# Second block's mixers: the recurrence between the projections, norm statistics per tile, norm weights in the columns, the FFN result per bank

## The reference

```
for layer in 0, 1:
    sh1, sc1, g1, sh2, sc2, g2 = split(silu(c) @ ada_w + ada_b)
    u = x * (1 + sc1) + sh1
    c_b, c_c, c_h, q, k, v, g, g_low = split(u @ w_in)        # 512 x3, 256 x2, 512 x2, 16
    y_conv = c_b * causal_conv3(c_c * c_h)
    gk = max(log_sigmoid(g_low @ gk_w2 + gk_b) / 16, -1);  b = cumsum(gk) in chunks of 64
    o  = (q e^b)(k e^-b)^T v, causal in the chunk, + (q e^b) state of the chunks before
    y_gla = rms(o) * gla_norm_w * silu(g)
    x = layernorm(alpha * x + (1 + g1) * [y_conv, y_gla] @ w_out) * ln1_g + ln1_b
    u = x * (1 + sc2) + sh2
    ff = dense SwiGLU, 2816 wide (layer 0)  or  8 experts of 2816, top 2 (layer 1)
    x = layernorm(alpha * x + (1 + g2) * ff) * ln2_g + ln2_b
```

## Time and profile before

| | us |
|---|---|
| median of 3 runs (lowest, highest) | 2401.27 (2396.63, 2406.88) |
| profiled execution, its own time | 2399.09 |
| its span | 2397.3 |
| layer 0's mixer, first transposes to first FFN matmul | 909.8 to 1094.5 |
| layer 0's FFN and norm, to the next transposes | 1094.5 to 1348.6 |
| layer 1's mixer, to the router | 1348.6 to 1536.0 |
| layer 1's experts, to the end | 1536.0 to 2397.3 |

### The profile page before, as it was taken

One profiled execution on the slowest core, in us unless ns is written; L12 is line 12 of the kernel. 1 busy time (PEld: TensorE's weight loads), 2 busy tenths in 40 slices (PEclk: granted clock), 3 DMA queues, 4 the chain that ended last, 5 costly groups with the idle time before them and its releaser, 6 DMA issues.

```text
span 2397.3 us, 68445 instructions
## 1 busy us (share of the span) xinstructions
PE 2180.4 (91%) x31915; PEld 1793.0 (75%) x31915; DVE 694.5 (29%) x1496; ACT 141.8 (6%) x270; POOL 160.6 (7%) x196
## 2 busy tenths in 40 slices
PE   5699989999999979988999797599999999999995
PEld 2478777777677768547777574399989989989894
DVE  7765342222222232144324414511010110101014
ACT  1102010000000000001000001100000000000000
POOL 8980000000000000000000000000000000000000
PEclk9899869999999978979999897799999999999997
DMA  9952567999999995316667431279999999989991
GB/s 343 320 184 107 187 234 276 395 395 394 393 393 394 395 376 182 118 53 229 238 225 269 150 123 57 88 263 348 342 342 346 386 334 339 371 303 383 329 340 39
DMA packets 304861, 658.13 MB, mean 275 GB/s; under 512 B 19844, under 2 KB 40852, under 8 KB 304660
## 3 DMA queue, kind: packets, MB, share of 16 engines
q1 hardware_dynamic: 295072, 646.99, 73.6%
q0 software_dynamic: 1456, 5.24, 0.7%
q10 hardware_dynamic: 8132, 2.72, 0.5%
HBM read 653.88 MB, written 1.05 MB: 273 GB/s over the span
## 4 chain that ended last, share of the span: by engine, by line
PE 80%; DMA 8%; DVE 6%; issue 4%; ACT 1%; SPq 1%; DVEq 0%; ACTq 0%
PE ps L1432 78%; DMA ring<-in_w_down_dram 8%; DVE arena L771 2%; PE ps L1440 2%; SPq L320 1%; DMA x<-in_x_dram 0%; ACT hT L543 0%; DVE stat L870 0%; DVE arena L1315 0%; ACTq L494 0%; DVE x L848 0%; DVE x L879 0%; DVE x L850 0%; DVEq L771 0%; DVE tok L796 0%
## 5 line engine op out<-in xcount | busy, mean ns | idle before, releaser
L1432 PE MATMUL ps<-arena,ring 128*64 128x96 f32 (+2 forms) x25216 | 990.7, 239 | 25.4 <-issue 23.3
L1432 PEld LDWEIGHTS ps<-arena,ring 128*64 128x64 f32 (+1 forms) x25216 | 972.0, 138 | 52.3 <-issue 45.3
L1432 PE MATMUL ps<-hT,ring 128*128 128x256 f32 x1616 | 353.1, 381 | 18.0 <-ACT hT L543 18.0
L1432 PEld LDWEIGHTS ps<-hT,ring 128*128 128x128 f32 x1616 | 307.6, 191 | 60.7 <-DVE stat L813 16.3
L1432 PE MATMUL ps<-ring,arena 128*64 128x512 f32 (+1 forms) x880 | 285.6, 616 | 16.9 <-DMA ring<-in_w_down_dram 14.4
L1432 PE MATMUL ps<-arena 128*128 128x128 f32 (+7 forms) x1296 | 244.5, 360 | 28.0 <-DVE arena L1143 11.4
L1168 DVE TENSOR_TENSOR arena<-arena,ps 128x384 f32<-128x384 f32 (+1 forms) x80 | 38.5, 481 | 760.2 <-PE ps L1432 760.2
L1432 PEld LDWEIGHTS ps<-ring,arena 128*64 128x64 f32 (+1 forms) x880 | 109.3, 165 | 175.2 <-issue 171.4
L1432 PEld LDWEIGHTS ps<-arena 128*128 128x128 f32 (+4 forms) x1296 | 167.3, 202 | 84.0 <-issue 52.7
L596 ACT ACTIVATE arena<-ps 128x384 f32<-128x384 f32 (+1 forms) x80 | 34.6, 432 | 1221.5 <-PE ps L1432 1221.5
L487 POOL DMA_DIRECT2D rowB<-in_ln_g_dram x4 | 2.1, 534 | 1357.4 <-DVE stat L1275 1017.4
(11 more groups left out here) (300 smaller groups left out, 859.3 us busy)
## 6 DMA issues: line engine op xcount, KB each, us to landing
ring<-in_moe_w_gate_dram SPq DMA_DIRECT2D x40, 2048.0 KB, 10.1
ring<-in_moe_w_up_dram SPq DMA_DIRECT2D x40, 2048.0 KB, 10.4
ring<-in_moe_w_down_dram SPq DMA_DIRECT2D x40, 2048.0 KB, 9.2
ring<-in_w_gate_dram SPq DMA_DIRECT2D x32, 2048.0 KB, 19.8
ring<-in_w_up_dram SPq DMA_DIRECT2D x32, 2048.0 KB, 19.7
ring<-in_w_down_dram SPq DMA_DIRECT2D x32, 2048.0 KB, 18.9
ring<-in_w_in_dram SPq DMA_DIRECT2D x18, 2048.0 KB, 10.4
ring<-in_w_ada_dram SPq DMA_DIRECT2D x12, 2048.0 KB, 20.9
```

The lines of the kernel that those rows point to most:

```text
L1432: ins = pe.matmul(*args, **kw)
```

## The change

- PE's order in the mixer: transposes, `glow_w`, the q/k slot, `gk_w2`, the `c_b` slot, the cumulative sums, the v slot, scores and states, the `c_c` and `c_h` slots, the recurrence's output, the g slot, the gate rows, `w_out`. DVE, ACT and SP (`C_IN2`) follow it. `conv` moves to other memory.
- `w_out`: both slots are taken at once and freed at once; the products go token tile by token tile, and `ya_ready` is counted per tile.
- Statistics of the layer norm are taken after each half tile of the residual sum (`normed_sum`); the transposes wait per token tile for `x_normed`, no longer for the columns; ACT waits for `scale_ready`.
- Layer 1's mixer norm has its gain and shift in the columns (`colC` has 7 vectors); `gain_x` comes after the transposes.
- The dense FFN: the last two `dense_down` are merged, bank by bank, each bank with a count `y_full`; DVE sums bank by bank, then `layer_norm`, then the columns `modT` and `y_free`.

```diff
-        C_IN2 = [(0, 512), (512, 1024), (1024, 1536), (1536, 2048), (2048, 2560), (2560, 3072)]
+        C_IN2 = [(1536, 2048), (0, 512), (2048, 2560), (512, 1024), (1024, 1536), (2560, 3072)]
...
+            def normed_sum(t, half, bank, gate):
+                cols = slice(half * CH, (half + 1) * CH)
+                step(dve.tensor_tensor(tok[:, t, cols], ps[:, bank, :], gB[:, gate, cols], ALU.mult))
+                step(dve.scalar_tensor_tensor(out=x[:, t, cols], in0=x[:, t, cols], scalar=ALPHA,
+                                              in1=tok[:, t, cols], op0=ALU.mult, op1=ALU.add))
+                step(stats(x, t, half), wait=t == half == 1)
...
                 for t in range(TT):
                     step(dve.tensor_scalar(v[:, t, :], v[:, t, :], stat[:, 108 + 2 * t:109 + 2 * t],
-                                           stat[:, 82 + t:83 + t], ALU.subtract, ALU.mult))
+                                           stat[:, 82 + t:83 + t], ALU.subtract, ALU.mult), done, wait=t == TT - 1)
...
+                for t in range(TT):
+                    for half in range(2):
+                        n = A_MIX[layer] + 6 + 2 * t + half
+                        dve.wait_ge(a_full, n + 1)
+                        normed_sum(t, half, 4 + n % 4, 0)
+                        dve.memset(stat[:, 122:123], 0.0).then_inc(a_free, 1)
...
-                    gain_x()
-                    step(dve.memset(stat[:, 121:122], 0.0), "rows_used")
-                    step(dve.tensor_scalar(scale_col[:, :], sec(SC2, 2), 1.0, None, ALU.add), "tokens_normed")
-                    transposed(scale_col, sec(SH2, 2))
+                    modulate(colC[:, 5, :], colC[:, 6, :], SC2, SH2, 2)
+                dve.wait_ge(a_free, A_MIX[layer] + 12)
...
+                    for t in range(TT):
+                        for half in range(2):
+                            dve.wait_ge(PH[1]["y_full"], 2 * t + half + 1)
+                            normed_sum(t, half, 2 * t + half, 1)
+                    layer_norm(D, x, LN_EPS, "x_normed")
                     dve.wait_ge(ada_cols, ADA_CHUNKS)
-                    dense_sum(PH[1], FFN_SEQ + 3 * len(W2), 0, None)
+                    step(dve.tensor_tensor(modT[:, 2, :], ps[:, 6, 0:48], colB[:, 48:96], ALU.add))
+                    dve.memset(stat[:, 122:123], 0.0).then_inc(PH[1]["y_free"], 1)
...
             def token_transposes(src, x_normed=None):
                 for t in range(TT):
+                    if x_normed is not None:
+                        pe.wait_ge(H["x_normed"], x_normed + t)
...
-                gates(layer + 1)
-                for c in range(3):
+                feature_major(glow_w, h_rhs, (0,), gv_(), cols=lambda f: 0, m=16).then_inc(v_full, 1)
+                def features():
                     s = take()
...
+                features()
...
+                features()
+                features()
...
+                cuts = [take(), take()]
+                pe.wait_ge(H["conv_ready"], layer + 1)
+                banks = [[ga_() for _ in cuts] for t in range(TT)]
...
+                    rows = [take(), take()]
+                    pe.wait_ge(PH[1]["hid_ready"], S2)
+                    for t in range(TT):
+                        for half in range(2):
+                            for u in (last_u - 1, last_u):
...
+                            last.then_inc(PH[1]["y_full"], 1)
+                    free(2)
```

More of the change, by code:

```diff
@@ L639, in _ @@
             for layer in range(2):
+                act.wait_ge(H["scale_ready"], 3 + 2 * layer)
                 transposed(shift_col)
-                for t in range(TT):
-                    bank = group()
-                    act.activation(sg_tok[:, t, :], ps[:, bank, :], ACT.Silu).then_inc(a_free, 1)
                 act.wait_ge(H["gk_abs"], layer + 1)
@@ L965, in _, with gated_sum @@
             ada_columns(2, 3)
-            def gated_sum(g, keep, cuts, a_groups=None):
-                for i, (c0, c1) in enumerate(cuts):
+            def gated_sum(g, keep, cuts):
+                for c0, c1 in cuts:
                     for t in range(TT):
[L972 to L981, removed]
                         b = group()
@@ L1306, in _ @@
                 step(dve.tensor_scalar(gk, gk, 1.0 / GK_DIV, GK_MIN, ALU.mult, ALU.max), "gk_ready")
[L1308 to L1320, removed]
+                for g in range(2):
+                    b = group()
+                    freed(dve.tensor_copy(cbT[:, 2 * g:2 * g + 2, :], bank2(b)))
+                for t in range(TT):
+                    b = group()
+                    freed_wait(dve.tensor_copy(v2[:, t, :], ps[:, b, :]))
+                dve.wait_ge(a_free, A_MIX[layer] + 4)
                 step(dve.scalar_tensor_tensor(out=q2T, in0=q2T, scalar=DK ** -0.5, in1=ebT, op0=ALU.mult, op1=ALU.mult),
@@ L1415, in _ @@
                     second_experts()
-                gated_ffn(ALPHA)
-                layer_norm(D, x, LN_EPS)
-                if layer == 1:
+                    gated_ffn(ALPHA)
+                    for t in range(TT):
+                        for half in range(2):
+                            ins = stats(x, t, half)
+                    step(ins)
+                    layer_norm(D, x, LN_EPS)
                     gain_x()
@@ L1939, in _ @@
                 free()
-                s = take()
-                for t in range(TT):
-                    token_major(h_lhs, slot(s, KD, CH), t, 0, CH, gv_()).then_inc(v_full, 1)
-                free()
-                s = take()
-                for t in range(TT):
-                    token_major(h_lhs, slot(s, KD, CH), t, 0, CH, ga_()).then_inc(a_full, 1)
-                pe.wait_ge(got_layer, 64 * (layer + 1))
-                feature_major(glow_w, h_rhs, (0,), gv_(), cols=lambda f: 0, m=16).then_inc(v_full, 1)
-                free()
                 pe.wait_ge(H["glow_ready"], layer + 1)
@@ L1968, in _ @@
                 last.then_inc(a_full, 1)
+                s = take()
+                for t in range(TT):
+                    token_major(h_lhs, slot(s, KD, CH), t, 0, CH, gv_()).then_inc(v_full, 1)
+                free()
                 pe.wait_ge(H["gla_in"], layer + 1)
@@ L2007, in _ @@
                     last.then_inc(v_full, 1)
-                projected = []
-                for c0, c1 in W_OUT_CUTS:
-                    s = take()
-                    for t in range(TT):
-                        bank = ga_()
+                s = take()
+                for t in range(TT):
+                    token_major(h_lhs, slot(s, KD, CH), t, 0, CH, ga_()).then_inc(a_full, 1)
+                free()
+                gates(layer + 1)
+                cuts = [take(), take()]
+                pe.wait_ge(H["conv_ready"], layer + 1)
+                banks = [[ga_() for _ in cuts] for t in range(TT)]
+                for t in range(TT):
+                    for half, s in enumerate(cuts):
                         for k in range(4):
-                            mm(ps[:, bank, 0:c1 - c0], cbT[:, k, t * P:(t + 1) * P], slot(s, KD, c1 - c0)[:, k, :],
+                            mm(ps[:, banks[t][half], :], cbT[:, k, t * P:(t + 1) * P], slot(s, KD, CH)[:, k, :],
                                start=(k == 0), stop=False, skip_group_check=True)
-                        projected.append((s, t, c1 - c0, bank))
                 for t in range(TT):
```

148 lines of the change are left out of this document (80 added, 68 removed).

## The result

The changed kernel took 2332.16 us (median of 4 runs, 2325.94 to 2340.74); the kernel before took 2399.03 beside it (4 runs, 2396.63 to 2406.88). The ratio is 0.9735, 95% interval 0.9702 to 0.9769: 66.9 us faster. The forecast was 2348. Two later repeats of the same kernel gave 2328.83 and 2333.88.

What follows compares the result with a forecast made beforehand. PE, busy 91% of the span, was taken to bound the kernel; savings of 20.2 (layer 0), 24.1 (layer 1) and 9.0 (FFN's end) sum to 53.3 us, giving 2348 us, range 2334 to 2367.

Steps and rivals of the forecast that it cites:

- (a): Mixer's decay gates: `glow_w` first, their chain hidden under the `c_b` slot; waits 6.0 and 0.7 go to 0, minus 6.7 a layer.
- (b): Recurrence's inputs: PE reaches `gla_in` right behind the v slot; pause 2.9 against 4.15, minus 1.3 us a layer.
- (d): `ya_ready` per tile: PE resumes after the first tile's copy; 0.45 left of 1.25, minus 0.8 us a layer.
- (e): DVE's head norm and convolution, 11.6 us, fit under the g slot's 13.9, later steps under `w_out`; nothing late, cost 0.
- (f): Norm at the mixer's end: idle time down to 6.0 us; minus 3.3 in layer 0, minus 8.0 in layer 1.
- (g): Clock around recurrence and `w_out`: output matmuls at full clock; minus 5.3 us a layer with a fall at `gla_in`, 10.2 without.
- (h): Mixer's start: transposes wait for `x_normed`, not the columns; minus 0.8 us in layer 0; `glow_w` taking over the slow clock: 0.
- rival 1: Clock holds over the pause at `gla_in` in both layers: 4.9 us more saved each, 2338; chance 0.24.
- 2: Small matmuls of scores, states and output lower the clock by themselves: saving only 38 us, 2363; chance 0.13.
- 3: Covers fail in part: DVE late with convolution or head norm, or late weight slots; gives back about 20 us, 2368; chance 0.15.
- 4: Slower than before: granted clock falls in the dense stretches; 2488 if half of the mixers' dense work were slow; chance 0.04.
- 5: A wait left in the order, such as `y_free`, restores an old pause; largest 9.0 us at the FFN, inside the range.

Runs made afterwards that it cites:

- the two combinations: Changed kernel with v slot first, tile 0 normed early, columns ahead of sums, early `y_free`; second also has columns before the FFN's last-bank wait: 2325.22, 2319.43 us.

## Why the prediction was right and where it failed

By its own steps, layer 0 (layer 1 where it differs):

| step | forecast | measured | from |
|---|---|---|---|
| (a) decay gates | 6.7 | 6.5 (6.9) | waits gone: 5.83 + 0.70 (6.20 + 0.70), where the prediction read 6.0 to 6.2 for the first |
| (b) `gla_in` | 1.3 | 1.5 (1.2) | 4.32 to 2.78 (4.00 to 2.78) |
| (c) before the output | 2.0 | 2.0 | wait gone |
| (d) `ya_ready` | 0.8 | 0.7 | 1.27 to 0.54 |
| (e) DVE's load | 0 | 0 | no DVE wait at the gate rows or within `w_out` |
| (f) norm | 3.3 (8.0) | 3.7 (8.0) | last `w_out` product to the FFN 15.06 to 11.32 (idle 14.04 to 6.03) |
| (g) clock, the places priced | 5.3 | 7.7 (7.4) | below |
| (h) start | 0.8 | 0.9 | idle 0.87 ahead of the transposes, gone |
| clock, places not priced | 0 | 3.4 (2.0) | below |
| FFN's end | 9.0 | 9.4, of which 1.7 went back at the FFN's start (2.9 in the two repeats) | 16.5 to 7.1 |

The starts themselves can't show (h): the mixer's first transposes begin anywhere from 904.0 to 912.0 in the profiles of the changed kernel and its variants. The idle piece of 0.87 is missing in all of them.

Every wait came out within half a microsecond of its working, so the way from rows of DVE to idle time of PE held: the pause at `gla_in` was put at 2.9 and is 2.78, the idle time before the transposes at 6.0 and is 6.03, behind the FFN at 7.3 and is 7.1. Removing them again one by one gave the prices back: 36 us for the order, 1.8 a norm for the statistics, 6.0 for `gain_x`, 7.4 to 8.9 for the FFN.

The step that failed is (g), the price of the clock, and it is a size, not a mechanism. It said: "I take it that the clock falls. Then scores and states keep their 5.0, and the next slot runs at half speed for a while." The clock did fall in both layers in every profile of the changed kernel. But it fell 1.7 us after PE had resumed, so scores and states took 3.61 (3.45 in layer 1), not 5.0: 1.4 to 1.6 a layer. The slots behind them lost 0.8, 1.0 and in other executions 2.4, of the 2.4 assumed. And `w_out`'s first half really gained its 2.2 to 2.5, which the forecast had set off against that loss. One part was sized too high: the output was to be halved, from 10.7 to 5.35, and took 6.21 at a clock of 1.00, so it gained 4.6. Layer 0 in sum: 4.6 + 2.5 + 1.4 - 0.8 = 7.7; in the two repeats, with 2.4 lost in the slots, 6.0. Forecast and rival 1 were thus the two ends, and the kernel lies between them: 6.0 to 7.7 between 5.3 and 10.2. The reasoning chose between "falls before work resumes" and "holds"; the row that could have told it more was its own 2.9 to 3 us of delay against a pause of 2.9, which leaves the time of the fall at the joint. The trace of before had more such rows: the clock fell 2.0, 2.2, 2.7 and 3.0 us after PE's last work at 1015.6, 1332.8, 1516.6 and 1079.5. At the twelve pauses at `gla_in` it fell 4.2 to 4.9 us after the last dense product, later than at any of these; why is open. The Trainium skill (TensorE: Matmul & The Clock Gate, Part 1: The HAM clock gate) says that the monitor's window runs free of the kernel; the identical program's 28.64 and 30.29 us agree with that. They don't prove it: the fall came within 0.7 us of the same place in all twelve, and only the time until the clock was back differed.

The second part of the miss is slow places that the forecast did not price. Before, the cumulative sums ran behind the gates' pause at half clock: 3.5 us from 1021.44 in layer 0, 3.8 in layer 1. They now take some 1.8, which is 1.7 and 2.0: a term that the forecast left out without a reason. The gate rows of layer 0 took 5.49 in front of `w_in` and take 3.7 later; the forecast had passed their slow clock on to `glow_w`, but there the clock came back at about 912.3, early enough. Before, it came near 918.6 (the window from 912 to 913 is still at 0.50, and at 0.85 after). This 1.7 is not luck: in all eleven profiles without the idle 0.87 the clock is back 2.8 to 3.3 us after the first transposes begin, where before it took 8.8. It isn't the new order either, since the run with the order put back has it too. So it belongs to the earlier start (h); as there is one profile of before and no run with that wait alone put back, this is argued and not shown. The loss at the FFN's start (0.64 over 1068.3 to 1072) isn't a chance of one trace either: its first slots take 29.55, 30.78 and 30.77 in the three profiles of the changed kernel, against 27.86 before. In the profile after, the mixers gain 10.1 more than forecast, less 1.5 at the FFN; in the two repeats 8.2 to 8.3, less 2.8.

The last 3.7 us came from the experts' stage, which the change touches only at its beginning (router to first dispatch 21.1 before, 20.9 after). They are not its gain. Over all profiled runs that stage lasted 842.4 to 866.2 us with no relation to the edit: 858.4 and 845.0 in the two repeats of the changed kernel, 861.3 in the kernel before. What varies is a pass over one expert's weights; two passes of the run after:

```profile
1608.05:1704.22 96.17, 96.17 (x2163) 93.38 (x2164) 11.42 (x22) 4.07 (x7) 0.00 (x0) 1.00 0.98 357
1901.82:2006.05 104.23, 98.78 (x2163) 95.32 (x2164) 11.45 (x22) 4.06 (x7) 0.00 (x0) 0.98 0.92 334
```

In the first, with loads at 357 GB/s, PE never waits. In the second it is idle for 5.4 us and its work takes 2.6 longer, at a clock of 0.98; the pass is 8 us longer and the rate over it 334. The bytes are nearly the same in both, so a longer pass gives a lower rate whatever its cause: that the loads are what varies is likely, but not shown. It is also why small effects were read from stages here, not from totals.

Of the rivals: 1 (the clock holds) was nearest in time, 2338, but not what happened, since the clock fell in each layer. 2 fell with the run with v first. 3 did not come: no wait for a ring slot or for DVE beyond those worked out. 4: the dense FFN ran at 1.00 over 1072 to 1308. 5: `y_free` is the FFN's last wait, at the size forecast.

Not shown by a run of their own: (d), (h) and the free ride of (e); no run puts one of them back alone.

## What to carry to other kernels

Where one engine bounds a kernel, put its dense work, not its small dependent work, behind each wait, and read what each pause costs twice: the idle time, and every slow row behind it, small ones included. A pause about as long as the delay after which the clock falls should be priced as a range, not as one of two cases; if it can be removed altogether, as by multiplying v earlier, the question goes away. When a saving of a few us is to be judged in a kernel with a stage that varies by 20, compare the stage and not the total.

## What was not expected of the hardware

- The clock can fall after work has resumed: about 4.4 us after the last dense product, 1.7 us into the scores (1.4 to 2.1 in twelve such places), behind a pause of 2.78 us in which it was 1.00. In the kernel before it fell 3 us after the last product of `w_out`.
- The same instructions at the same pause gave 28.64, 30.29 and 30.28 us for two slots; the clock was down for 3.4 us in the first (973.7 to 977.2) and 6.8 in the second (976.5 to 983.4).
- Small matmuls straight behind dense ones kept the clock at 1.00 (2.73 us for the 40 of scores and states; 3.61 and 4.99 behind pauses of 2.78 and 5.04).
- The same product behind much the same pause can be fast or slow: layer 1's `glow_w` took 3.61 us in the changed kernel's three profiles, behind one idle piece of 6.3, and 5.64 behind the same 6.28 with v first. It took 5.10 behind 8.13, and 5.18 and 6.56 in the two combinations, where idle time and transposes alternate. What decides it no run shows.
